# Gate/up products ahead of the last down product in every pair of experts, loaded in 4 MB transfers

## The reference

```
def swiglu(x, wg, wu, wd):
    return (jax.nn.silu(x @ wg) * (x @ wu)) @ wd
...
    y = routed_experts(xf, top_idx, top_w, w_gate, w_up, w_down) + swiglu(xf, ws_gate, ws_up, ws_down)
...
        x = layer_norm(DEEPNORM_ALPHA * x + ffn, ln2_g[l], ln2_b[l])
```

## Time and profile before

| | |
|---|---|
| median of 3 runs | 1187.65 us (1187.37 to 1188.17) |
| profiled execution | 1188.19 us |
| its span, first to last instruction | 1186.4 us |
| TensorE busy | 1148.7 us (97%) |
| VectorE, ScalarE busy | 352.7 us (30%), 255.3 us (22%) |
| read from HBM, written | 452.22 MB, 3.15 MB; 384 GB/s over the span |
| mean granted TensorE clock | 0.996 of full speed |

### The profile page before, as it was taken

The page is one execution under the profiler, slowest core; times in us unless marked ns, Lnnn a source line. Parts: engine busy times, 40 slices in busy tenths (PEclk is TensorE's granted clock), DMA queues, the critical chain, the costliest instruction groups (busy, mean ns, idle before and its releaser), DMA issues.

```text
span 1186.4 us, 15935 instructions
## 1 busy us (share of the span) xinstructions
PE 1148.7 (97%) x6752; PEld 523.0 (44%) x6752; DVE 352.7 (30%) x1053; ACT 255.3 (22%) x511; POOL 8.4 (1%) x20
## 2 busy tenths in 40 slices
PE   8999999999999999999999999999999999999995
PEld 7774633433343333333386655333343334333331
DVE  0424722222222222222333346232222222222224
ACT  1132421222122211111112323221222122112111
POOL 0000000000000000000000000000000000000001
PEclk9999999999999999999999999999999999999998
DMA  9982599999999999999998626999999999999995
GB/s 378 421 328 113 213 415 425 428 427 426 428 426 427 428 427 428 427 427 428 413 425 360 252 80 254 412 428 428 426 429 426 428 427 426 429 426 428 426 425 224
DMA packets 39952, 456.49 MB, mean 385 GB/s; under 512 B 4416, under 2 KB 4544, under 8 KB 8256
## 3 DMA queue, kind: packets, MB, share of 16 engines
q1 hardware_dynamic: 39872, 455.38, 91.5%
HBM read 452.22 MB, written 3.15 MB: 384 GB/s over the span
## 4 chain that ended last, share of the span: by engine, by line
PE 76%; DMA 21%; DVE 2%; issue 0%; ACT 0%; POOL 0%; POOLq 0%; DVEq 0%
PE bank L705 29%; DMA slots<-in_w_gu 20%; PE bank L725 14%; PE bank L926 5%; PE bank L854 5%; PE bank L607 4%; PE bank L634 4%; PE bank L863 2%; PE bank L1052 2%; PE bank L825 1%; PE bank L713 1%; PE bank L829 1%; PE bank L873 1%; PE bank L883 1%; PE bank L959 1%; PE bank L619 1%
## 5 line engine op out<-in xcount | busy, mean ns | idle before, releaser
L705 PE MATMUL bank<-slots,front 128*64 128x512 f32 x2048 | 456.0, 595 | 13.6 <-DMA slots<-in_w_gu 13.5
L705 PEld LDWEIGHTS bank<-slots,front 128*64 128x64 f32 x2048 | 139.9, 137 | 280.8 <-issue 249.4
L725 PE MATMUL bank<-slots,r 128*32 128x512 f32 x2016 | 229.9, 595 | 1.1 <-issue 1.1
L1403 DVE SCALAR_TENSOR_TENSOR yparts<-bank,small,yparts 128x512 fp32r<-128x512 f32 x128 | 96.0, 750 | 265.4 <-ACT yparts L1086 265.4
L1086 ACT ACTIVATE yparts<-bank,small 128x512 fp32r<-128x512 f32 x128 | 87.9, 687 | 239.8 <-PE bank L725 239.8
L1395 DVE TENSOR_TENSOR high<-high,bank 128x256 f32<-128x256 f32 x64 | 26.9, 421 | 354.5 <-ACT high L1113 326.7
L725 PEld LDWEIGHTS bank<-slots,r 128*32 128x32 f32 x2016 | 59.3, 109 | 137.2 <-issue 135.7
L1113 ACT ACTIVATE high<-bank 128x256 f32<-128x256 f32 x60 | 23.0, 384 | 413.1 <-PE bank L705 413.1
L1086 ACT ACTIVATE front<-bank 128x512 f32<-128x512 f32 (+1 forms) x161 | 84.5, 580 | 88.7 <-PE bank L825 28.2
L607 PEld LDWEIGHTS bank<-selr,xparts 128*128 128x128 f32 x512 | 64.3, 188 | 45.4 <-issue 45.4
L634 PE MATMUL bank<-yparts 64*128 64x512 f32 x512 | 79.4, 421 | 1.9 <-DVE yparts L1403 1.9
(11 more groups left out here) (123 smaller groups left out, 616.6 us busy)
## 6 DMA issues: line engine op xcount, KB each, us to landing
slots<-in_w_gu SPq DMA_DIRECT2D x116, 2048.0 KB, 30.8
slots<-in_w_dn SPq DMA_DIRECT2D x58, 2048.0 KB, 27.5
slots<-in_dense SPq DMA_DIRECT2D x28, 1024.0 KB, 14.8
slots<-in_w_gu SPq DMA_DIRECT2D x24, 1024.0 KB, 9.0
slots<-in_w_dn SPq DMA_DIRECT2D x10, 1024.0 KB, 37.4
slots<-in_first SPq DMA_DIRECT2D x3, 768.0 KB, 7.0
r<-in_pool_mat SPq DMA_DIRECT2D x2, 1024.0 KB, 25.9
sdn<-in_shared_dn SPq DMA_DIRECT2D x2, 1024.0 KB, 10.0
```

The lines of the kernel that those rows point to most:

```text
L705: m = pe.matmul(H[64 * a:64 * a + 64, :], cells[:, cell(B, k, j), a, :], GU[g][:, a, :, k, :], start=k == 0, stop=k == KD - 1)
L725: m = pe.matmul(Y[half][r0:r0 + 32, :], hT[:, kc * P + 64 * a + 32 * t:kc * P + 64 * a + 32 * t + 32], wd[:, a, kc, :], start=kc == 0, sto ...
L1403: dve.scalar_tensor_tensor(ysp[:, 1, half * 512:(half + 1) * 512], Y[half][:, :], wslot[:, b:b + 1], ysp[:, 0, half * 512:(half + 1) * 512 ...
```

## The change

1. **Order on TensorE.** Every pair, not only the last two, now runs `gate_up` of q, then both halves of `down` of q-1 (`down_both`), then `turn_h` of q, and then gather, combine, gather, combine, with a wait for `lo` in front of each. ScalarE's `hi` and VectorE's `lo` of pair q-1 move behind the silu and the multiplication of pair q. `last_two` is gone.
2. **Order of the transfers.** The down weights of pair q-1 are started after the gate/up weights of pair q (`give_dn`). Those of pairs 30 and 31 stay in halves of 1 MB.
3. **Size.** The gate/up weights of pairs 6 to 29 (the seventh to the thirtieth) come in one transfer of 4 MB, released by `h_full` alone; the product waits for all of it before its first matmul.
4. **Shared expert.** Its four down products move from pairs 26 to 29 to pairs 14 to 17 (the 15th to the 18th).
5. **Pair 2** (the third). The second gate/up half comes as two quarters of 1 MB: the first is released by `sgu_rd`, after k = 0 to 3 of the shared expert's second tile, the second by `sh1` as before, and the transfer ahead into xs now stands between them.
6. The wait for the block's last two gathered pieces (`g_sb`) moves from the start of a block's first product to its last two steps.

```diff
+SHARED = PAIRS // 2 - 2
+WHOLE = range(6, PAIRS - 2)
...
+                def give_dn(q):
+                    sp.wait_ge(ps.y_full, 2 * (base + q - 2))
+                    if round_ is None and q >= PAIRS - 2:
+                        for a, done in ((0, half_in[q - PAIRS + 2]), (KF * D, ps.w_in[2][q % 3])):
+                            sp.dma_start(slots[:, q % 3, 2 * W_CHUNK + a:2 * W_CHUNK + a + KF * D],
+                                         w_dn[l * PAIRS + q][:, a:a + KF * D]).then_inc(done, 16)
+                    else:
+                        load_dn(ps, l, q, q % 3)
...
+                    elif round_ is None and q in WHOLE:
+                        sp.wait_ge(ps.h_full, n - 2)
+                        sp.dma_start(slots[:, g, 0:2 * W_CHUNK], w_gu[l * PAIRS + q]).then_inc(ps.w_in[1][g], 16)
                     else:
                         sp.wait_ge(ps.h_half, n - 2)
                         load_gu(ps, l, q, g, (0,))
                         sp.wait_ge(ps.h_full, n - 2)
                         load_gu(ps, l, q, g, (1,))
-                    sp.wait_ge(ps.y_full, 2 * (n - 2))
-                    load_dn(ps, l, q, g)
+                    if q > 3:
+                        give_dn(q - 1)
...
+                give_dn(PAIRS - 1)
...
-                sp.wait_ge(*full_at(l, "sh1"))
-                load_gu(main, l, 2, 2, (1,))
+                a, m, z = W_CHUNK, W_CHUNK + W_CHUNK // 2, 2 * W_CHUNK
+                sp.wait_ge(sgu_rd, l + 1)
+                sp.dma_start(slots[:, 2, a:m], w_gu[l * PAIRS + 2][:, a:m]).then_inc(third_in, 16)
                 sp.wait_ge(split_rd, 2 * l + 2)
                 sp.wait_ge(*full_at(l, "xTb3"))
                 sp.wait_ge(spill_out, 16 * l + 16)
                 sp.dma_start(xs[:].rearrange("p t d -> p (t d)"), w_dn[l * PAIRS + SPLIT][:, 0:KF * D]).then_inc(ahead_in, 16)
+                sp.wait_ge(*full_at(l, "sh1"))
+                sp.dma_start(slots[:, 2, m:z], w_gu[l * PAIRS + 2][:, m:z]).then_inc(main.w_in[1][2], 16)
...
+                            if k or (round_ is None and q in WHOLE):
+                                pe.wait_ge(ps.w_in[1][g], (turn * USES[g] + use) * 16 + 16)
...
+                    gate_up(n, q, g, use, first)
+                    if first:
...
+                    else:
+                        down_both(n - 1, q - 1, (q - 1) % 3, (q - 1) // 3)
+                        turn_h(n)
+                        begins = l if q == 1 and round_ is None else None
+                        if filling:
+                            refill(0)
+                        combine(ps, n - 1, 1 - b, 0, begins)
+                        if filling:
+                            refill(1)
+                        if not last:
+                            combine(ps, n - 1, 1 - b, 1, begins)
...
-                        if round_ is None and q >= PAIRS - 6:
-                            i = q - (PAIRS - 6)
+                        if round_ is None and SHARED <= q < SHARED + 4:
+                            i = q - SHARED
                             shared_down(l, i // 2, i % 2)
```

More of the change, by code:

```diff
@@ L47 @@
 SPLIT = 3
+SHARED = PAIRS // 2 - 2
+WHOLE = range(6, PAIRS - 2)
+HALVES = [[q for q in range(g, PAIRS, 3) if q not in WHOLE] for g in range(3)]
 FIRST = (0, 1, 2, 4, 6, 8)
@@ L321, in build @@
         quarter_rd = sem("quarter_rd")
+        sgu_rd = sem("sgu_rd")
+        third_in = sem("third_in")
         quarter_in = [[sem(f"quarter_in{i}_{h}") for h in range(2)] for i in range(3)]
@@ L388, in pairs_of_pass @@
         def pairs_of_pass(base, body, start=0, ahead=None):
-            for q in range(start, PAIRS if ahead is None else PAIRS - 2):
+            for q in range(start, PAIRS):
                 body(base + q, q, q % 3, q % 2, q // 3, q == 0, q == PAIRS - 1)
@@ L690, in gate_up @@
                     B, j = q // SPAN, q % SPAN
+                    if j == 0 and B:
+                        pe.wait_ge(ps.g_sb, first_fill + KD * B + KD - 2)
                     if not first:
@@ L699, in gate_up @@
                             m.then_inc(ps.h_half, 1)
+                        if k >= KD - 2 and j == 0 and B:
+                            pe.wait_ge(ps.g_sb, first_fill + KD * B + k + 1)
                         if k % 4 == 0:
+                            if round_ is None and q == 2 and k:
+                                pe.wait_ge(third_in, 16 * l + 16)
                             if round_ is None and 3 <= q < 6:
                                 pe.wait_ge(quarter_in[g][k // 4], 16 * l + 16)
-                            pe.wait_ge(ps.w_in[k // 4][g], (turn * USES[g] + use) * 16 + 16)
+                            if k or (round_ is None and q in WHOLE):
+                                pe.wait_ge(ps.w_in[1][g], (turn * USES[g] + use) * 16 + 16)
+                            elif round_ is None:
+                                pe.wait_ge(ps.w_in[0][g], (turn * len(HALVES[g]) + HALVES[g].index(q)) * 16 + 16)
+                            else:
+                                pe.wait_ge(ps.w_in[0][g], (turn * USES[g] + use) * 16 + 16)
                         for a in range(2):
@@ L727, in down, with down_both @@
                     m.then_inc(ps.y_full, 1)
+                def down_both(n, q, g, use):
+                    pe.wait_ge(ps.hT_sb, n + 1)
+                    B, j = q // SPAN, q % SPAN
+                    main_last = round_ is None and q >= PAIRS - 2
+                    if round_ is None and q == SPLIT:
+                        pe.wait_ge(ahead_in, 16 * l + 16)
+                    for half in range(2):
+                        if main_last and half == 0:
+                            pe.wait_ge(half_in[q - PAIRS + 2], 16 * l + 16)
+                        else:
+                            pe.wait_ge(ps.w_in[2][g], (turn * USES[g] + use) * 16 + 16)
+                        if B + 1 < BLOCKS:
+                            pe.wait_ge(ps.g_sb, first_fill + KD * (B + 1) + 2 * j + half + 1)
+                        else:
+                            pe.wait_ge(ps.lo_rd, 2 * n - 1 + half)
+                        down(q, g, half)
+                        if half == 0 and q == PAIRS - 1:
+                            combine(ps, n - 1, 0, 1)
                 def body(n, q, g, b, use, first, last):
@@ L732, in body @@
                     filling = B + 1 < BLOCKS
-                    fills = first_fill + KD * (B + 1) + 2 * j
-                    if j == 0 and B:
-                        pe.wait_ge(ps.g_sb, first_fill + KD * (B + 1))
-                    gate_up(n, q, g, use, first)
[L737 to L749, removed]
+                    def refill(i):
+                        if i == 0 and j == 0:
+                            pe.wait_ge(ps.sel_rd, first_block + B + 2)
+                        if not first:
+                            pe.wait_ge(ps.lo_rd, 2 * n - 1 + i)
+                        gather(ps, 2 * j + i, Y[i])
+                    gate_up(n, q, g, use, first)
@@ L750, in body @@
+                    if first:
+                        refill(0)
+                        refill(1)
+                        if round_ is None:
+                            shared_turn(l, 1)
+                        turn_h(n)
+                    else:
+                        down_both(n - 1, q - 1, (q - 1) % 3, (q - 1) // 3)
+                        turn_h(n)
                         begins = l if q == 1 and round_ is None else None
                         if filling:
-                            combine(ps, n - 1, 1 - b, 0, begins)
@@ L768, in body @@
                         turn_sel(ps, q + 1)
-                        if round_ is None and q >= PAIRS - 6:
-                            i = q - (PAIRS - 6)
+                        if round_ is None and SHARED <= q < SHARED + 4:
+                            i = q - SHARED
                             shared_down(l, i // 2, i % 2)
[L773 to L798, removed]
                 pairs_of_pass(base, body, 0, (lambda: load_count(pe, l)) if round_ is None else None)
-                if round_ is None:
-                    last_two()
+                down_both(base + PAIRS - 1, PAIRS - 1, (PAIRS - 1) % 3, (PAIRS - 1) // 3)
                 m = combine(ps, base + PAIRS - 1, 1, 0)
@@ L1055, in shared_up @@
                         filled(l, f"sh{t}", m)
+                    elif t == 1:
+                        m.then_inc(sgu_rd, 1)
                 turn_tile(0)
@@ L1109, in run @@
                     g_out(0, k, bank[FIRST_BANKS[k] if round_ is None else 4 + k % 4])
[L1111 to L1120, removed]
                 def hi(n, b):
@@ L1127, in hi, with body @@
                             .then_inc(ps.hi_rd, 1)
-                pairs_of_pass(base, body, 0, (lambda: load_count(act, l)) if round_ is None else None)
[L1129 to L1135, removed]
+                def body(n, q, g, b, use, first, last):
+                    act.wait_ge(ps.h_full, n + 1)
```

(24 more changed lines are left out.)

16 lines of the change are left out of this document (2 added, 14 removed).

## The result

The changed kernel takes 1194.82 us (median of 4 runs, 1194.62 to 1195.04) against 1187.51 for the kernel before beside it: a ratio of 1.0061 (95% interval 1.0048 to 1.0074), 7.3 us slower. I had forecast 1187.1 and a range up to 1191.0.

The account below looks back on a forecast made before the run. The landing of each layer's last gate/up half, set by the transfer stream, was taken to bound the kernel. Terms +2.2, -3.1 and +0.4 gave -0.5 us on the profiled 1188.19, so a median of 1187.1 us, range 1183.8 to 1191.0.

Parts of the forecast that it names:

- step 1: Order on TensorE: a wait for `lo` makes a pair 13.57 us instead of 13.27, costing nothing where the stream bounds.
- Step 2: Pair 2's earlier quarter: pair 3's first quarter lands 2.3 to 2.9 us earlier; whether that lasts is left to Step 3.
- Step 3: Pair 6's 4 MB, released by product 3's end: the stream runs dry, 1.1 us later a layer, +2.2 us in two.
- Step 4: Stream rate with 4 MB transfers: 0.064 us gained for each of 48 transfers fewer, -3.1 us, bounds 0 and -6.2.
- Step 5: Moved shared products: costed at nothing; left in place with large transfers, TensorE would be some 4 us late at pair 31.
- the signs of the stream: Expected in the profile: traffic from 141 us, low GB/s between 189 and 193 us, windows of 429 to 431 GB/s.
- Step 6: End of the layer: product 31's first half ends 0.1 us before the landing; uneven landings cost +0.4 us together.
- A: 4 MB transfers (32 KB rows) bring no rate: 1190.3 us, slower; chance 0.18.
- D: Product 31 starts late because pair 29's 4 MB land 1.4 us late, in both layers: 1189.6 us, slower; chance 0.10.

Follow-up runs that it names:

- experiment 3: Kernel before with the second 1 MB of the down weights of pairs 6 to 29 not loaded: 1170.53 us, ratio 0.9859.
- experiment 1: Changed kernel with the gate/up weights of pairs 6 to 29 in two 2 MB transfers again: 1195.33 us, ratio to the kernel before 1.0068.
- experiment 2: Changed kernel with the second 1 MB of the down weights of pairs 6 to 29 not loaded: 1195.71 us.
- experiment 4: Kernel before with the new order of products and transfers and the later `g_sb` wait; halves, shared products and pair 2 unchanged: 1195.08 us, ratio 1.0064.
- experiment 8: Kernel before with the shared products in pairs 14 to 17 and pair 2's quarters, nothing else: 1190.08 us, ratio 1.0020.
- experiment 9: Kernel before, shared products moved, pair 2's three 1 MB transfers all released by `sh1`: 1188.12 us, ratio 1.0007; beside it the early start again: 1189.54 us, 1.0015.
- experiment 10: Kernel before with 4 MB transfers: pairs 7 to 27 with shared products moved, 1185.1 us (0.9973); pairs 6 to 29 with nothing else, 1192.28 us (1.0041).
- experiment 6: Kernel before with only the shared down products moved from pairs 26 to 29 to 14 to 17: 1186.96 us, ratio 1.0000.

## Why the prediction was wrong

**The step that failed is step 1**, where it says that the new order costs nothing in the stage bound by the stream, since "14.7 - 13.57 is still 1.1 us of cover". That cover exists only once TensorE has caught up with the stream. It starts a layer with three filled slots, and before, it waits for a transfer only from pair 21 on, about 8.5 us a layer; in pairs 1 to 20 every added tenth goes into its own schedule. I compared rates and never added up TensorE's whole layer. The sum was at hand: 27 pairs by 0.3 are 8.1 us, nearly all of those waits.

What the traces give is more. From product 1 to product 28 a pair of layer 0 takes 13.70 us, against 13.25 in the old order with the light stream (experiment 3; shared products taken off): unrounded 0.445, which by 27 is 12.0 us. Pairs 28 to 30 take 13.01 against 12.81, 0.6 us more. With small differences at product 1 that is 12.6 a layer. The waits that it replaces are 9.1 in layer 0 and 8.7 in layer 1, which leaves 3.4 and 3.7; the first product stands 0.7 earlier, and 6.4 us is the difference of the two profiled spans (1192.8 and 1186.4). The medians are 7.3 apart. Experiments 1 to 4 show the cause: less stream, same time; order alone, same loss.

**The size of the term**: 0.3 taken, 0.43 measured, inside the bounds of 0.05 and 0.5, but partly by luck. `lo` ends 1.55 us behind down (181.15 to 182.70) and not 1.8, and of a wait in front of the second gather the rows show about 0.1. The larger part is that gathers and combines each take longer in the new order (0.65 to 0.69 for 0.53, 0.66 for 0.57), a term that the prediction put at nothing with "The same instructions run in the new order, so the work stays 13.27 us". With 0.3 the failure would have been hidden: TensorE and stream nearly even.

**Step 2** was right as to the landing (measured from product 0, 2.3 us earlier in the changed kernel and 2.8 in experiment 8; 2.3 to 2.9 written) and wrong as to what lies behind it: in the changed kernel the window from 152 to 175 us has 405 GB/s, before it was above 420. In the changed kernel it is of no account, since TensorE sets the time. In the old order it costs 2 to 3 us, together with the split of the half (experiments 8 and 9).

**Step 3** was right in mechanism and size: one hole, behind 190 us, and 204.3 for the landing. It too is of no account in this kernel (experiment 1), which I had at +2.2 us.

**Step 4** was right: 429 against 427 GB/s, and 2.7 us for 42 transfers fewer (experiment 10). The rule of the Trainium skill (SBUF — State Buffer, "The DMA setup-cost knee"), about 2 us fixed for each transfer, would give an estimate of 84 us for them; the measurement decides, and gives 0.064 each while the queue is full. The changed kernel gets nothing from it, because its stream is ahead anyway.

**Step 5** was right in the old order: nothing by itself (experiment 6), 7 us apart with the large transfers (experiment 10; 21 against 24 pairs of them, so not a pure pair), of which 3.3 to 3.5 us a layer is a late product 31, where some 4 was written. Its sign for the changed kernel, TensorE waiting for the stream in pairs 22 to 29, failed: there is no such wait. It was the one sign that spoke of TensorE's lead; the signs of the stream nearly all came true beside a wrong time.

**Step 6** did not come to bear: product 31 starts after the last half has landed. Its printed terms add up to 29.6 us, which is 0.1 behind the landing at 29.5 and not before it; measured, two pairs of 13.01 and 3.5 us are 29.5. The rows that it takes from the earlier trace rows are second halves of products 25 and 28 (16 matmuls each), which leaves its 45.59 us as they are.

**The rivals.** A and D had the right sign and the wrong cause. The true one, TensorE becoming the limit of the whole layer, was none of mine. D named TensorE but only at pair 31, on a transfer that comes late.

## What to carry to other kernels

Where a fast engine starts behind a buffered lead of the stream and catches up with it late, the spare time of that engine is its total wait in the layer, not the difference of the two rates times the number of steps: add up its whole schedule before costing anything at nothing. Leaving out some of the transfers gives that floor in one run, and it should be known before an order is changed. Larger transfers paid a little here (2.7 us for 42 fewer), and only where something covered their later first use.

## What the runs showed that was not expected

With the early start of pair 2, pair 3's quarters went to a nearly empty queue. Its second quarter landed 4.1 us behind the first instead of 2.5, and 20 us of such traffic ran at 359 and 368 GB/s with the engines counted as 98% and 97% busy. The earlier start, with the split into three transfers, made the whole kernel 0.15 to 0.20% slower. And windows with rows of 8, 16 and 32 KB a partition show 422, 427 and 429 to 430 GB/s.
